# Expert loop of a decoder step: the next expert's eight row transposes moved in front of 12 products, directly behind four transposes of the activation

## What is computed

```python
def moe(x, w_router, b_router, w_gate_up, b_gate_up, w_down, b_down):
...
    def expert_block(args):
        xb, e = args
        h = xb @ w_gate_up[e] + b_gate_up[e]
        gate = jnp.minimum(h[:, 0::2], SWIGLU_LIMIT)
        up = jnp.clip(h[:, 1::2], -SWIGLU_LIMIT, SWIGLU_LIMIT)
        glu = gate * jax.nn.sigmoid(gate * SWIGLU_ALPHA)
        return ((up + 1.0) * glu) @ w_down[e] + b_down[e]
...
```

## Time and profile before

| | us |
|---|---|
| median of 3 executions | 1428.47 |
| lowest and highest | 1428.11, 1431.58 |
| span of the profiled execution | 1427.3 |
| TensorE busy in it | 1404.2 (98%) |
| VectorE busy | 1185.9 (83%) |
| ScalarE busy | 991.8 (69%) |
| GpSimd busy | 399.0 (28%) |

### The profile page before, as it was taken

The page is one execution under the profiler, slowest core; times in us unless marked ns, Lnnn a source line. Parts: engine busy times, 40 slices in busy tenths (PEclk is TensorE's granted clock), DMA queues, the critical chain, the costliest instruction groups (busy, mean ns, idle before and its releaser), DMA issues.

```text
span 1427.3 us, 18390 instructions
## 1 busy us (share of the span) xinstructions
PE 1404.2 (98%) x6675; PEld 1021.3 (72%) x6675; DVE 1185.9 (83%) x1081; ACT 991.8 (69%) x954; POOL 399.0 (28%) x231
## 2 busy tenths in 40 slices
PE   9999999999999999999999999999999999999995
PEld 6876754777777777777777777777777777777773
DVE  3164455899999999999999999999999999999996
ACT  3134422777777777777777777777777777777774
POOL 2012121443555664222222222222222222222203
PEclk9999999899999999999999999999999999999998
DMA  9640065599999999999999999999999999999984
GB/s 367 206 152 16 35 229 217 193 382 355 375 383 372 362 358 353 369 379 384 372 376 367 365 374 358 372 368 366 368 372 366 379 365 362 374 368 372 367 302 147
DMA packets 52260, 461.94 MB, mean 324 GB/s; under 512 B 11369, under 2 KB 15435, under 8 KB 26489
## 3 DMA queue, kind: packets, MB, share of 16 engines
q1 hardware_dynamic: 39641, 437.77, 79.3%
q0 software_dynamic: 10624, 20.42, 6.6%
q10 hardware_dynamic: 1936, 2.99, 0.7%
HBM read 447.41 MB, written 24.31 MB: 331 GB/s over the span
## 4 chain that ended last, share of the span: by engine, by line
PE 94%; DVE 2%; DMA 1%; issue 1%; POOL 1%; ACT 1%; POOLq 0%; SPq 0%; DVEq 0%; ACTq 0%
PE psum L2270 25%; PE psum L2271 25%; PE psum L2272 24%; PE psum L1879 7%; PE psum L2040 4%; PE psum L2283 2%; PE psum L2254 2%; PE psum L2265 2%; PE psum L1849 1%; DMA ring<-in_w_mem_kv 1%; POOL small L761 0%; ACT ring L836 0%; DMA area<-hn_tbl,idx_i 0%; PE psum L1950 0%; PE psum L1974 0%
## 5 line engine op out<-in xcount | busy, mean ns | idle before, releaser
L1608 DVE TENSOR_TENSOR low<-raw,high 128x2048 fp32r<-128x2048 f32 x384 | 865.4, 2284 | 43.3 <-ACT high L1026 42.4
L1026 ACT CAST high<-raw 128x2048 fp32r<-128x2048 f32 x384 | 725.1, 1913 | 91.3 <-PE psum L2272 88.6
L2270 PE MATMUL psum<-high,area_r 128*104 128x512 f32 x1536 | 610.4, 397 | 0.9 <-DVE area_r L1677 0.9
L2271 PE MATMUL psum<-high,area_r 128*104 128x512 f32 x1536 | 603.3, 393 | 0.0
L2272 PE MATMUL psum<-low,area_r 128*104 128x512 f32 x1536 | 602.6, 392 | 0.0
L2272 PEld LDWEIGHTS psum<-low,area_r 128*104 128x104 f32 x1536 | 257.6, 168 | 97.1
L2270 PEld LDWEIGHTS psum<-high,area_r 128*104 128x104 f32 x1536 | 257.8, 168 | 91.7 <-DVE area_r L1677 1.3
L2271 PEld LDWEIGHTS psum<-high,area_r 128*104 128x104 f32 x1536 | 258.2, 168 | 90.3
L679 POOL DMA_INDIRECT area<-hn_tbl,idx_i x32 | 158.4, 4949 | 95.0 <-DVE idx_i L1575 72.3
L644 POOL CAST pick_r<-area 64x104 fp32r (+1 forms) x33 | 30.4, 921 | 460.8 <-PE psum L2272 460.6
L692 POOL DMA_INDIRECT y_tbl<-area,idx_i x31 | 61.7, 1991 | 222.4 <-ACT area L1036 199.7
(11 more groups left out here) (261 smaller groups left out, 901.7 us busy)
## 6 DMA issues: line engine op xcount, KB each, us to landing
raw<-in_w_gate_up SPq DMA_DIRECT2D x128, 2048.0 KB, 10.8
raw<-in_w_down SPq DMA_DIRECT2D x64, 2048.0 KB, 10.4
ring<-in_w_in SPq DMA_DIRECT2D x7, 1024.0 KB, 21.1
area<-in_w_out SPq DMA_DIRECT2D x1, 4096.0 KB, 30.4
ring<-in_w_mem_kv SPq DMA_DIRECT2D x2, 1024.0 KB, 9.4
area<-in_x_prompt SPq DMA_DIRECT2D x4, 512.0 KB, 11.7
ring<-in_mem_kT SPq DMA_DIRECT2D x1, 2048.0 KB, 10.1
ring<-in_cache_mem_v SPq DMA_DIRECT2D x1, 2048.0 KB, 8.3
```

What stands on the lines that cost most here:

```text
L1026: nc.scalar.copy(high_w(i), raw_w(t)).then_inc(sem("w_high"), 1)
L1608: v.tensor_tensor(low_w(t), raw_w(t), high_w(i), ALU.subtract).then_inc(sem("w_low"), 1)
L2270: mm(bank, high, wh, start=start, stop=False)
L2271: mm(bank, low, wh, start=False, stop=False)
```

## The change

In TensorE's `period`, `x_rows(n + 1)` stands in front of `gate_up(n, 5)` instead of behind it. Nothing else is changed on any engine, and all waits stay as they are. TensorE's order was: half 4, four transposes of the activation, half 5, eight transposes of the next rows, half 6. It is now: half 4, four transposes, eight transposes, half 5, half 6. The last period has no `x_rows`.

```diff
@@ -2348,9 +2348,9 @@
                     pe.wait_ge(sem("bias_row"), 2 * early + 4)
                 gate_up(n, 4, last, k)
                 act_rows(n, 0, overflow)
-                gate_up(n, 5, last, k)
                 if not last:
                     x_rows(n + 1, k + 1)
+                gate_up(n, 5, last, k)
                 wait(pe, "yrow_ready", n * 2)
                 down(n, 6, last)
                 down(n, 7, last, middle=last)
```

## The result

| | before | after |
|---|---|---|
| median of 6 executions, us | 1428.86 | 1438.30 |
| lowest and highest | 1428.11, 1431.58 | 1432.26, 1441.24 |
| ratio, 95% interval | | 1.0057 [1.0041, 1.0073] |
| span of the profiled execution | 1427.3 | 1436.7 (own time 1438.44) |

The medians are 9.4 us apart, and so are the spans. The ratio on record, 1.0057, is not the quotient of the two medians (1.0066); by it the change costs 0.57%, 8.1 us. The same holds for the ratios of the experiments. The forecast was 1428.7 in 1425.9 to 1431.6: the result is outside, on the slow side. The executions also spread more than before, by 9.0 us instead of 3.5.

A forecast was written before the change was run, and what follows sets the result against it. TensorE, busy 98% of the span, was taken as the bound. Seams -0.3 us and early lag +0.5 us gave +0.2 us on the profiled execution; against the runs' median the forecast was 1428.7 us, range 1425.9 to 1431.6.

The forecast's parts named there:

- the seams: Where TensorE's products give way to transposes and back: two groups joined save 0.01 us in each of 31 periods, -0.3 us.
- The joined group: TensorE's four and eight transposes in one row: 1.02 us from the first to the product behind.
- The early lag: Periods 0 and 1: VectorE, without idle time, is 0.48 us late and TensorE waits for act_low, +0.5 us.
- The gate step's idle: ScalarE's L1042 waiting for half 5 in a steady period: 0.47 + 0.71 = 1.18 us.
- Low part 9: VectorE's L1608 ahead of its product in a steady period: 0.7 us late, margin near 0.7 us left, cost 0.
- the gather wait: TensorE's moved transposes wait for the gathered rows: closest in period 0, 9.5 us left, cost 0.
- The queue: SP's and GpSimd's queues: nothing is moved past anything, they only hear later of a used half.
- transposes wait for the gather: Rival: TensorE's transposes are earlier in the queue but wait for the gather, once 1 us, 1429.7 us; chance 0.01.
- the second rival: VectorE's lag reaches TensorE in every period, at low part 9's product: +9.6 us, 1438 us; chance 0.05.

The follow-up runs named there:

- the run whose rows need no gather: Changed kernel, but in periods 0 to 7 the rows' transposes read constants and don't wait for the gather: 1430.89 us, ratio 1.0004 against the kernel before.
- Period 1 alone: Kernel before with the new order of transposes and half 5 only in period 1: 1432.38 us, ratio 1.0014.
- periods 2 to 4 alone: Kernel before with the new order of transposes and half 5 only in periods 2, 3 and 4: 1431.77 us, ratio 1.0018.
- the late periods alone: Kernel before with the new order only from period 8 on: 1431.70 us against 1430.43, ratio 1.0005.
- changed kernel again: The changed kernel without further edits, measured a second time, in four executions: 1439.98 us, ratio 1.0079 against the kernel before.
- early periods alone: Kernel before with the new order only in periods 0 to 7: 1436.35 us, ratio 1.0049.

## Why the prediction was wrong

**What held.** TensorE has no slack, and the seams are worth almost nothing: 0.31 us over 18 periods is 0.017 each, predicted 0.01. (By the weight-load rule of the Trainium skill, TensorE: Matmul & The Clock Gate, Part 3, "The mechanism", two seams fewer should have freed visible time; neither nor any period after agrees.) The joined group takes 1.01 us from its first transpose to the product behind (835.77 to 836.78), forecast 1.02. The early lag came out at 0.43 us for 0.5, in the run whose rows need no gather. The steady period went by the working, as the changed kernel's ScalarE and VectorE in period 15 show:

```profile
839.81 0.69 ACT L1042 ACTIVATE area<-psum,cst 104x512 f32<-104x512 f32 x1 [1.16 <-PE psum L2272]
```

```profile
840.92 1.09 DVE L1672 TENSOR_TENSOR area_r<-psum,area_r 128x416 fp32r<-128x416 f32 x2 [0.42 <-ACT area_r L1057]
...
845.45 4.49 DVE L1608 TENSOR_TENSOR low<-raw,high 128x2048 fp32r<-128x2048 f32 x2
849.86 0.58 DVE L1677 TENSOR_TENSOR area_r<-psum,area_r 128x416 fp32r<-128x416 f32 x1
```

The gate step's idle is 1.16 (forecast 1.18). Low part 9 ends at 847.7 and its product starts at 848.45: margin 0.7, as forecast. act_low ends at 850.44, product 851.29.

**The step that failed** is the gather wait, "They wait for the gather. The closest pair is in period 0 [...] Cost 0". It was wrong in three ways.
- *The pair.* Period 0's is not the closest. Period 1's gather ran from 305.55 for 9.76 us, its transposes at 326.46. I looked at one gather and took it for the tightest because it was the first.
- *The clock to count from.* I set a load's 10.8 us from the instruction's start, and only where there were 9.5 us to spare. In the changed kernel's trace the gathers issued in periods 1 and later land behind the *end* of their instruction, by 10.7 us in the median of 30 (4.3 to 12.2). With the same 10.8 counted from there, period 1 gives 315.31 + 10.8 = 326.1 against transposes at 326.46 - 2.8 = 323.7: a wait of 2.4 us. In the profiles of the kernels with the new order there it was 1.3 to 3.4. The rows of the instruction and of the transposes were in the trace of the kernel before; only the landing was not.
- *The queue.* "Nothing is moved past anything on SP's and GpSimd's queues; they only hear later of a used half." True of the order, but GpSimd's instructions change their length with what VectorE does beside them, and about half of the loss, period 4's 5.05 us, is that. "They only hear later of a used half" was the cause, put down as a reason for no cost.

The rival "transposes wait for the gather" was thus the true mechanism, with a chance of 0.01, priced at once 1 us; it was three waits, 7.2 us of idle, and 1.6 of slow products. VectorE's lag does reach TensorE, by GpSimd's queue and a gather, not by the low parts that the second rival named.

**What adds up, and what stays open.** Period 1 alone gives 0.14%, periods 2 to 4 alone 0.18%; the changed kernel 0.57 and 0.79% in two measurements. In its profile the difference is longer waits, in period 1 (3.4 us against 1.7 with period 1 alone) and in period 4 (3.4 against 2.2), the half clock behind the second, and period 9's 0.97. Why the waits are longer when both periods have the new order was not tried, nor why they differ by some 1 us from run to run (3.4 and 2.2 in period 1, 3.4 and 2.6 in period 4, in two profiles of the changed kernel; that this makes the spread of its executions is likely, and not shown). In period 9 the gather for expert 10 goes out 20.4 us ahead of the activation's transposes and takes 9.35 us as an instruction, with the late periods alone as well as in the changed kernel; only its landing differs, 10.0 us behind the instruction's end with the late periods alone (1.5 us before it is needed) and 12.2 in the changed kernel. What sets the time from the instruction's end to landing is not shown: it was 5.0 us in period 0 and anything from 4.3 to 12.2 later.

## What to carry to other kernels

Before a consumer is moved earlier, list the slack of every instance of what it waits for, counted to the landing of the data and not to the end of the instruction that issued it: the first and the steady one may be fine and the second not. A small delay on an engine with time to spare is still a change: ask which short stops of it another engine lived on. GpSimd's DMA instructions are such a tenant, and a queue of them carries the delay to a load that is due almost 50 us later.

## What was not expected of the hardware

**The length of GpSimd's DMA instructions follows VectorE's subtractions.** The same gather of 104 rows took from 1.29 to 9.76 us as an instruction. Twelve profiles (both kernels and all experiments) fall into two groups by the gather for expert 4, 4.58 or 7.39 us, and in each of them the next gather follows at 36.5 or 44.5 us; a stop of VectorE of 0.15 us in the right place is enough for the short one. But a stop is not what it takes. In the twelve profiles all 336 gathers from expert 4 on end 0.97 to 1.01 us behind the end of a VectorE instruction that reads two operands from SBUF (L1608 or L1566). Behind 79 of these VectorE stops; behind 252 it goes straight on to L1677, which reads one operand from PSUM; and behind 5 (the gather for expert 10, in the kernel before and four experiments) the next L1608 follows at once. From the kernel before, both without a stop:

```profile
591.09 8.89 DVE L1608 TENSOR_TENSOR low<-raw,high 128x2048 fp32r<-128x2048 f32 x4
591.50 2.86 POOL L679 DMA_INDIRECT area<-hn_tbl,idx_i  x1 [0.90 <-POOL area L671]
...
621.85 5.23 POOL L679 DMA_INDIRECT area<-hn_tbl,idx_i  x1 [0.86 <-POOL area L671]
626.13 0.59 DVE L1677 TENSOR_TENSOR area_r<-psum,area_r 128x416 fp32r<-128x416 f32 x1
```

The first ends at 594.36, 0.99 behind the first of the four; where half 5 of period 8 is reported late the same gather sits through all four and takes 9.35 us. The second ends at 627.08, 0.98 behind the last L1608 before L1677. When a gather gets in between two subtractions and when it does not is not shown. The Trainium skill (SBUF — State Buffer, "SBUF: two separate sides") describes an exclusive lock on a port pair that VectorE and GpSimd share, taken by VectorE's instructions with two operands in SBUF against a GpSimd instruction that reads SBUF, as L1608 and L679 are. The trace agrees that GpSimd is held while L1608 runs, as the 336 gathers above show, and that L1677, with one operand in PSUM, lets it go on.

**The clock behind a wait.** In the changed kernel's trace the wait of period 4 (3.4 us) was followed by products at 1.2 GHz, that of period 1 (3.4 us too) was not. In other runs, waits of 2.6 us (changed kernel again) and 2.9 us (early periods alone), both in period 4, were followed by a fall of the clock that began already in the eight transposes (1.34 and 1.06 us from the first to the product behind, for 0.71) and took in the first four and six products; waits of 0.9 to 2.2 us by none. So a shorter wait cost clock where a longer one did not, and what tells them apart was not tried.
